# The second pooling input tile of a block, placed behind the pooling products of the block before

## The reference, cut to what matters

```python
proj = h @ w_in
z, xbc, dt_raw, u, gates = jnp.split(proj, split_at, axis=-1)
# scan, per group, per chunk of 128 tokens: y = y_diag + y_off + d_skip * x; y = y * silu(z); RMS norm; @ w_out
# pooling, four groups of 256 channels, windows 2, 4, 8, 16:
outs.append((csum - shifted) / count - ug)          # trailing mean minus the token itself
mixed = jnp.einsum("bsgi,gio->bsgo", pooled, w_group)
y_pool = mixed * scale
x = x + (g_ssd * y_ssd + g_pool * y_pool) @ w_mix_out
```

## Time and profile before

| | |
|---|---|
| median of 3 runs | 1859.26 us (1857.36 to 1859.41) |
| the profiled execution | 1857.28 us, of which 1855.5 us span |
| PE busy | 1810.7 us, 98% of the span |
| DVE, ACT, POOL busy | 1409.3, 1177.7, 351.1 us |
| the last group's blocks | about 324 to 386 us |
| gate tiles up to the first `SO` tile | about 386 to 416 us |

### The profile page before, as it was taken

The page is one execution under the profiler, slowest core; times in us unless marked ns, Lnnn a source line. Parts: engine busy times, 40 slices in busy tenths (PEclk is TensorE's granted clock), DMA queues, the critical chain, the costliest instruction groups (busy, mean ns, idle before and its releaser), DMA issues.

```text
span 1855.5 us, 25121 instructions
## 1 busy us (share of the span) xinstructions
PE 1810.7 (98%) x8997; PEld 1504.2 (81%) x8997; DVE 1409.3 (76%) x1027; ACT 1177.7 (63%) x936; POOL 351.1 (19%) x327
## 2 busy tenths in 40 slices
PE   7999999999999999999999999999999999999997
PEld 6888888678889878888888888888888888888776
DVE  4576676553334788889889889899889888988964
ACT  4655565342232577777777777777777777777764
POOL 5223324530000502111111111111211211111000
PEclk9999999999999999999999999999999999999999
DMA  6434443343346299999999999999999999999941
GB/s 184 117 101 103 114 129 101 106 142 85 97 132 265 83 388 363 366 379 367 364 377 363 373 373 376 370 371 377 369 368 382 368 363 378 369 364 378 356 151 46
DMA packets 152888, 503.71 MB, mean 271 GB/s; under 512 B 15290, under 2 KB 75362, under 8 KB 119204
## 3 DMA queue, kind: packets, MB, share of 16 engines
q1 hardware_dynamic: 140916, 478.10, 69.5%
q0 software_dynamic: 11872, 24.83, 5.6%
q10 hardware_dynamic: 48, 0.07, 0.0%
HBM read 493.28 MB, written 25.90 MB: 280 GB/s over the span
## 4 chain that ended last, share of the span: by engine, by line
PE 84%; DVE 4%; POOL 4%; ACT 4%; issue 3%; DMA 1%; SPq 0%; POOLq 0%; DVEq 0%; ACTq 0%
PE gu_ps L2088 24%; PE dn_ps L2103 13%; PE gu_ps L2092 12%; PE gu_ps L1856 7%; PE gu_ps L1858 7%; PE gu_ps L1857 7%; PE dn_ps L2109 6%; PE et_ps L2074 3%; PE gu_ps L2256 1%; PE gu_ps L2079 1%; ACT w_hi L894 1%; PE gu_ps L1878 1%; POOL win L797 1%; POOL dx L783 1%; POOL slot_rows L822 1%
## 5 line engine op out<-in xcount | busy, mean ns | idle before, releaser
L1677 DVE TENSOR_TENSOR split_l<-ring,split_h 128x2048 fp32r<-128x2048 f32 x384 | 868.2, 2288 | 111.5 <-ACT split_h L1160 108.6
L1160 ACT ACTIVATE split_h<-ring 128x2048 fp32r<-128x2048 f32 x384 | 727.7, 1916 | 164.6 <-PE gu_ps L2092 123.9
L2088 PE MATMUL gu_ps<-split_h,xgT_h 128*128 128x512 f32 x992 | 274.8, 399 | 0.0
L2092 PE MATMUL gu_ps<-split_l,xgT_h 128*128 128x512 f32 x992 | 265.5, 389 | 0.0
L2088 PE MATMUL gu_ps<-split_h,xgT_l 128*128 128x512 f32 x992 | 265.4, 389 | 0.0
L2088 PEld LDWEIGHTS gu_ps<-split_h,xgT_l 128*128 128x128 f32 x992 | 186.2, 188 | 39.4
L2092 PEld LDWEIGHTS gu_ps<-split_l,xgT_h 128*128 128x128 f32 x992 | 186.2, 188 | 39.1
L2088 PEld LDWEIGHTS gu_ps<-split_h,xgT_h 128*128 128x128 f32 x992 | 184.1, 188 | 38.8
L1337 DVE TENSOR_TENSOR w_lo<-w_raw,w_hi 128x2048 fp32r<-128x2048 f32 (+1 forms) x45 | 102.8, 2285 | 142.7 <-ACT w_hi L894 130.1
L810 POOL COPY icur<-slots 128x1 int32 (+1 forms) x31 | 53.0, 1711 | 691.9 <-PE et_ps L2074 691.9
L2103 PE MATMUL dn_ps<-split_h,actT_h 128*128 128x512 f32 x512 | 161.2, 396 | 4.7 <-issue 4.7
(11 more groups left out here) (339 smaller groups left out, 2601.0 us busy)
## 6 DMA issues: line engine op xcount, KB each, us to landing
ring<-in_w_gate_up SPq DMA_DIRECT2D x256, 1024.0 KB, 7.2
ring<-in_w_down SPq DMA_DIRECT2D x128, 1024.0 KB, 8.2
w_raw<-in_w_in SPq DMA_DIRECT2D x28, 1024.0 KB, 5.8
arow<-acum_rows POOLq DMA_DIRECT2D x16, 512.0 KB, 6.4
w_raw<-in_w_ssd_out SPq DMA_DIRECT2D x8, 1024.0 KB, 5.8
w_raw<-in_w_in SPq DMA_DIRECT2D x9, 512.0 KB, 6.6
w_raw<-in_w_mix_out SPq DMA_DIRECT2D x4, 1024.0 KB, 8.7
wpg<-in_w_ple_gate SPq DMA_DIRECT2D x2, 2048.0 KB, 20.6
```

Source lines behind the costliest of these rows:

```text
L1160: a.activation(split_h[s % SPLIT][:, :], ring[s % RING][:, :], ACT.Copy).then_inc(hi_done, 1)
L1677: v.tensor_tensor(split_l[s % SPLIT][:, :], ring[s % RING][:, :], split_h[s % SPLIT][:, :].bitcast(F32), ALU.subtract).then_inc(lo_done, 1)
L2088: t.matmul(gu_ps[:, b * 512:b * 512 + 512], x[:, k, :], split_h[s][:, b * 512:b * 512 + 512], start=False, stop=False)
L2092: o = t.matmul(gu_ps[:, b * 512:b * 512 + 512], xgT_h[:, k, :], split_l[s][:, b * 512:b * 512 + 512], start=False, stop=k == KD - 1)
```

## The change

One line: the order of the filler tiles in a block of the last group.

```diff
--- before.py
+++ after.py
@@ -108,7 +108,7 @@
-    return [("U", c, 0), ("U", c, 1)] + ([("PO", c - 1, 0), ("PO", c - 1, 1)] if c else [])
+    return [("U", c, 0)] + ([("PO", c - 1, 0), ("PO", c - 1, 1)] if c else []) + [("U", c, 1)]
```

## The result

The changed kernel takes 1869.68 us (median of 4 runs, 1866.73 to 1872.42) against 1858.34 us (1857.36 to 1859.41): ratio 1.0058, 95% interval 1.0046 to 1.007, so 11.3 us slower. The forecast was 1865.2 us and slower. The direction was right; the time lies 0.7 us beyond the upper end of the range and the loss is nearly double the 5.9 us. The 0.7 us are less than the 5.7 us between the lowest and the highest of the four times, so on which side of the range's end the median fell was partly chance; the loss itself was not.

What follows compares the result with a forecast made beforehand. PE's work and a loop through the other engines were taken to bound the last group nearly equally. The late U1 copies and DVE's normalisation gave +5.9 us, carried whole: 1859.26 + 5.9 = 1865.2 us, range 1862.0 to 1869.0.

Steps and rivals of the forecast that it cites:

- Two paths: Last scan group: PE's own work, 18.3 us a block, and a loop through the other engines, 17.4 and 19.8 us.
- ring: Last group: DVE's step output, POOL's mask and sum, ACT's U1 copy, next output; forecast late by 4.09, 7.05, 7.41 us.
- The new wait: PE idle before U1 until ACT, behind `decay`, copies PO0: some 3.6 and 3.2 us in blocks 1 and 2.
- The seam: Behind the blocks, transposes wait for DVE's normalised rows: +5.9 us, between 4.74 (PE alone) and 7.41.
- The hidden work: Weight rounding and fetches behind U1's copy come 4 to 9 us later, pooling weights land in 2.8; costed at nothing.
- The clock: Rival: PE's clock falls to half after the new idle times, 1.7 us each, giving 1866.9 or 1868.6 us; chance 0.20.
- The range: Whole time 1862.0 to 1869.0 us, from PE's bound of 4.74 us up to one or two clock falls.
- The short wait: Rival: ACT empties PO0 right behind PO1, PE loses 1 us a block, at best -1.9 us, 1857.4; chance 0.06.
- absorbed behind: Rival: later stages behind the blocks hide part of the delay, only 1 to 3.7 us stay, near 1862; chance 0.12.

Runs made afterwards that it cites:

- filled kernel: Changed kernel plus 26 unread matmuls on PE between PO1 and U1 in blocks 1 and 2: 1864.81 us, ratio 1.0026 to the kernel before.
- Block 1 alone: The new filler order in block 1 only, blocks 2 and 3 as in the kernel before: 1875.44 against 1871.62 us, ratio 1.0027.
- second job's chip: The unaltered changed kernel measured again on another chip: 1868.42 us against 1860.11 for the kernel before, ratio 1.0045.
- the last kernel: Kernel before, with step products around the PO tiles on PE and DVE's last weight difference moved into y_norm: 1859.05 against 1859.63 us, ratio 0.9995.
- the step's products first: Kernel before, with PE doing the step's own products ahead of the PO tiles: 1868.84 against 1871.62 us, ratio 0.999; repeated, 1.000.

## Why the prediction was right or wrong

- **What bounds the kernel: right.** Two paths of nearly equal length. The filled kernel follows the sum of ring and PE to 0.1, 0.2 and 0.4 us at the three steps. (The ring's third round, 393.13 - 372.50 = 20.6 us, was left out where its rounds were listed; the sum does use its pieces.)
- **The new wait: right in kind, a little short.** It is PO0's bank, released by ACT behind `decay`; 3.77 and 3.56 us for 3.6 and 3.2 forecast, 0.93 in block 3. Part of the difference is the restart: from the start of `decay` to U1 it takes 343.24 - 341.47 = 1.77 us, not 1.63. With `decay` moved the wait shrinks to 0.93 everywhere and all but 0.9 us of the loss is gone.
- **The seam: right.** +6.3 for +5.9, decided by the normalisation on DVE. The new order in block 3 alone costs 1.3 us there.
- **The hidden work: right that it costs nothing, too small in its sizes.** In the changed kernel, counted from `cb`, ACT's rounding of block 1 comes 6.6 us later, and the three fetches behind U1 come 10.2, 12.8 and 13.8 us later instead of 4 to 9. The pooling weights, now issued 0.4 us behind a fetch, take 6.2 to 7.2 us to land and not 2.8: those for PO0 of block 2 are there at 351.77 + 7.2 = 359.0, and PO0 starts at 360.35. PE's waits of 300 to 480 us show none for a DMA, ACT's rounding or DVE's difference, but the cover was 1.4 us and not the 5.8 us that the forecast had.
- **The clock: wrong, and this is the step that failed.** It stood as a rival with a chance of 0.20 and 1.7 us a fall, and was left out of the sum. The clock fell behind both long waits in both profiles of the changed kernel, and a fall cost 1.64 to 2.4 us; together 3.3 to 4.05 us. The sign that the prediction had named, 12 matmuls in 4.4 us behind a new wait and not in 2.72, came: 5.20 and 4.09 us in the first profile, 4.43 and 4.41 in the second. The two bounds at hand (2.83 us without a fall, 4.69 us with one) gave no ground for so low a chance, as both new waits lay between them. Block 1 alone shows that length does not decide there, since 3.77 us passed without a fall and 3.14 us did not. The Trainium skill, "TensorE: Matmul & The Clock Gate", "Why this matters for your kernels", advises against idle gaps of this size. The traces agree in five of the six waits above 3 us that the new order brought in three profiles (3.77 and 3.56 twice, 3.77 and 3.14), but not in the sixth. What makes the clock fall behind one wait of 3.77 us and not behind another stays open.
- **The range** ended at 1869.0; two falls of 1.7 us and nothing beside make 1868.6. With 6.3 us and two falls of 1.64 to 2.4 the stretch costs 9.6 to 10.4, 1868.9 to 1869.7 on the median of before that the forecast started from. The measured median is 1869.68. On the second job's chip the changed kernel's loss was 8.4 us by its ratio (5.8 to 11.0), with a median of 1868.42.
- **Rivals.** The short wait did not come, for the reason given (the mask ends too late); nothing was absorbed behind, since the delay at the first SO tile, 11.24 us in absolute time, is 11.23 us at the first matmul of the mixing output 150 us later (579.62 against 568.39).

## What to carry to other kernels

With two alternating buffers, moving one job changes who releases the buffer of the next; look at what stands in the releasing engine's queue at that moment, not only at how long it takes to empty the buffer. A move of PE work that brings a wait of about 3 us or more is better priced with a fall of TensorE's clock in the forecast itself, here 1.6 to 2.4 us each, and with a range that also holds the case without one. And where two paths end within 2 us of each other, shortening one alone gains at most that gap.

## What the runs showed of the hardware beside

The same wait of PE in the expert stage, for L1683, takes 2.81 to 2.98 us in ten of the eleven profiles, whatever the kernel, and the clock behind it differs: it stays up in three (before twice, the changed kernel on the second chip), falls for a while in four and for longer in three, the first profile of the changed kernel among them. Two of them, the kernel before on the second chip and the last kernel (L2079: four matmuls in 1.03 us, or in 1.89):

```profile
665.54 1.03 PE L2079 MATMUL gu_ps<-bparts,sel 96*128 96x512 bf16 x4 [2.83 <-DVE xgT_l L1683]
```

```profile
663.89 1.89 PE L2088 MATMUL gu_ps<-bparts,sel 96*128 96x512 bf16 x4 [2.97 <-DVE xgT_l L1686]
```

In the one profile where this wait is 3.65 us long (the step's products first, first job) the clock stayed up. From this wait's end to the end of the next one, of 4.69 us, the same work takes 1100.8 us without a fall (four profiles), 1102.4 with the short one (four) and 1103.7 with the long one (three): the falls cost 1.6 and 2.9 us. Behind the 4.69 us the clock is at half in all eleven, and behind the 2.6 us in front of PO1 of block 1, in the three profiles that have it, it never falls. So in these runs the length of an idle stretch of about 3 us does not decide whether the clock falls.

The long fall alone set the first profile of the changed kernel back by 2.9 us (676.72 against 665.33 at this wait, 1780.46 against 1766.15 at the next one), which is more than the differences of 0.1% that the last experiments looked for.
